# First modulation by output quarters, layer 0 queries and keys accumulated between them, second attention's scores two units ahead

## The reference, cut to what matters

```python
c_act = jax.nn.silu(c)
for l in range(DEPTH):                                   # DEPTH = 2
    mod = c_act @ ada_w[l] + ada_b[l]                    # [1024] @ [1024, 6144]
    sh_m, sc_m, g_m, sh_f, sc_f, g_f = jnp.split(mod[:, None, :], 6, axis=-1)
    h = _rmsnorm(x, norm_mix[l]) * (1 + sc_m) + sh_m
    proj = h @ w_in[l]                                   # queries qa, keys ka, values va, latents, gates, ...
    ...                                                  # attention with a table of relative biases,
    ...                                                  # latent attention, state space scan
    x = x + g_m * (merged @ w_out[l])
    h = _rmsnorm(x, norm_ffn[l]) * (1 + sc_f) + sh_f
    ...                                                  # gated feed-forward net with a convolution
# second block: two attentions with 8 heads of 64, then 32 experts, top 2 of one group, then a norm
```

## Time and profile before

| | |
|---|---|
| time, median of 3 runs | 1949.88 us (1947.15 to 1951.94) |
| the profiled execution's own time | 1946.01 us |
| its span in the profile | 1944.2 us |
| PE busy | 1864.6 us, 96% |
| DVE, ACT busy | 628.2 us (32%), 418.7 us (22%) |
| HBM read | 440.11 MB |
| mean granted PE clock | 0.983 |

### The profile page before, as it was taken

One profiled execution on the slowest core, in us unless ns is written; L12 is line 12 of the kernel. 1 busy time (PEld: TensorE's weight loads), 2 busy tenths in 40 slices (PEclk: granted clock), 3 DMA queues, 4 the chain that ended last, 5 costly groups with the idle time before them and its releaser, 6 DMA issues.

```text
span 1944.2 us, 20225 instructions
## 1 busy us (share of the span) xinstructions
PE 1864.6 (96%) x8628; PEld 1304.4 (67%) x8628; DVE 628.2 (32%) x1139; ACT 418.7 (22%) x888; POOL 0.8 (0%) x9
## 2 busy tenths in 40 slices
PE   6999999999999999999999999999889999999996
PEld 2477787888888648788888888865764444444432
DVE  4352267333232335127642232034441111111112
ACT  3253122212110234312212111012421011011112
POOL 0000000000000000000000000000000000000000
PEclk8999999999999999999999999999989999999999
DMA  9753364264446665337245453453329999999993
GB/s 388 266 168 125 130 218 154 105 216 156 147 161 229 215 216 174 130 111 274 92 161 185 132 171 136 141 216 130 135 82 406 428 428 427 427 427 427 428 427 128
DMA packets 137433, 443.25 MB, mean 228 GB/s; under 512 B 8832, under 2 KB 58240, under 8 KB 123520
## 3 DMA queue, kind: packets, MB, share of 16 engines
q1 hardware_dynamic: 134912, 438.26, 59.6%
q10 hardware_dynamic: 2432, 3.71, 0.6%
HBM read 440.11 MB, written 1.84 MB: 227 GB/s over the span
## 4 chain that ended last, share of the span: by engine, by line
PE 91%; DVE 4%; ACT 2%; DMA 1%; issue 1%; DVEq 1%; PEldq 0%; SPq 0%; ACTq 0%; PEld 0%
PE acc L705 36%; PE acc L1147 11%; PE acc L715 10%; PE aux L1186 6%; PE aux L980 4%; PE acc L980 4%; PE acc L1134 3%; PE acc L1001 3%; PE acc L1195 2%; PE aux L641 2%; PE aux L1195 2%; DMA ring<-in_ada_first 1%; PE acc L956 1%; PE aux L651 1%; PE aux L804 1%; ACT area L1269 1%
## 5 line engine op out<-in xcount | busy, mean ns | idle before, releaser
L705 PE MATMUL acc<-hT,ring 128*128 128x256 f32 x2688 | 592.2, 382 | 7.1 <-ACT hT L1342 7.1
L705 PEld LDWEIGHTS acc<-hT,ring 128*128 128x128 f32 x2688 | 513.2, 192 | 80.6 <-issue 12.0
L715 PE MATMUL acc<-ring,hT 128*128 128x512 f32 (+1 forms) x384 | 165.5, 591 | 5.3 <-ACT hT L1342 5.3
L1147 PE MATMUL acc<-ring,yT 128*64 128x512 f32 x512 | 169.2, 594 | 0.0
L2098 DVE SCALAR_TENSOR_TENSOR area<-acc,vectors,area 128x255 f32<-128x255 f32 (+1 forms) x176 | 72.7, 476 | 214.1 <-ACT area L1522 212.5
L715 PEld LDWEIGHTS acc<-ring,hT 128*128 128x128 f32 x384 | 73.7, 194 | 90.6 <-issue 88.4
L2336 DVE TENSOR_TENSOR xT<-xT,acc 128x1024 f32<-128x1024 f32 x17 | 20.8, 1222 | 292.3 <-PE acc L1195 292.3
L1724 DVE SCALAR_TENSOR_TENSOR ring<-ring,cspread 128x1024 f32<-128x1024 f32 x80 | 93.2, 1221 | 63.3 <-DMA ring<-in_ada_rest 63.3
L1147 PE MATMUL acc<-area,yT 128*64 128x512 f32 x384 | 112.9, 594 | 0.0
L1147 PEld LDWEIGHTS acc<-ring,yT 128*64 128x64 f32 x512 | 52.4, 137 | 74.5 <-issue 74.5
L1269 ACT ACTIVATE area<-aux 128x512 f32<-128x512 f32 (+3 forms) x65 | 41.4, 676 | 230.7 <-PE aux L641 225.1
(11 more groups left out here) (379 smaller groups left out, 1951.8 us busy)
## 6 DMA issues: line engine op xcount, KB each, us to landing
ring<-in_w_in SPq DMA_DIRECT2D x34, 2048.0 KB, 9.6
ring<-in_ffn_w_up SPq DMA_DIRECT2D x44, 1024.0 KB, 7.7
ring<-in_ada_rest SPq DMA_DIRECT2D x20, 2048.0 KB, 8.0
ring<-in_w_up SPq DMA_DIRECT2D x17, 2048.0 KB, 18.8
ring<-in_w_down SPq DMA_DIRECT2D x17, 2048.0 KB, 18.4
ring<-in_w_gate SPq DMA_DIRECT2D x16, 2048.0 KB, 15.6
area<-in_w_up SPq DMA_DIRECT2D x12, 2048.0 KB, 19.2
area<-in_w_down SPq DMA_DIRECT2D x12, 2048.0 KB, 17.8
```

Source lines behind the costliest of these rows:

```text
L705: mm = pe.matmul(acc[LU.buf[use]][:, SEQ * j:SEQ * j + SEQ], w[:, k, c0:c0 + P], x[:, k, :], start=(k == 0), stop=(k == n - 1))
L715: mm = pe.matmul(acc[LU.buf[use]][:, at:at + width], x[:, k, P * t:P * t + P], w[:, k, :], start=(k == 0), stop=(k == n - 1))
L1147: mm = pe.matmul(dst[CAP * e:CAP * e + CAP, :], xg[:, b, k, CAP * e:CAP * e + CAP], w[:, k, :], start=(k == 0), stop=(k == KT - 1))
```

## The change

Three parts.

1. `ada_first` is laid out anew so that its four loads split the *outputs*: load i has all eight input tiles for 256 columns of `sh_m` and the same 256 of `sc_m`. Each load so gives the shift and scale of feature tiles 2i and 2i + 1 by itself. PE's `first_block` has as many matmuls per load as before, into `aux2`, and a drain after each; `first_block_sums` has four matmuls of one column each per load, where there were four of four columns in all. DVE's `first_gains(i)` does copy, sums, gains and two tiles of `hT`; ACT's `first_shift(i)` adds two shifts.
2. The loads of `q` and `k` come between those of the first two blocks, in slots 2 and 3, and blocks 2 and 3 reuse slots 0 and 1 after blocks 0 and 1. `first_quarter(name, i)` accumulates input tiles 2i and 2i + 1 of `q` or `k` in their accumulators, in an order written out on PE among blocks, bias groups and sums. `v` and `ada4` are next in slots 0 and 1. The rest of `CHUNKS` keeps its order with the slots turned by two. The bias groups use `aux`, the first norm sum `acc[1]`. Two DMA issues of ACT (`rows`, `cspread`) move behind `first_shift(1)`. What ACT does after the last shift stays.
3. In the second attention PE issues `scores(u + 2)` after the transposes of unit u, where it issued `scores(u + 1)` ahead of them, and DVE takes the largest of unit u + 1 before it waits for the exponential of unit u.

```diff
-... "ada_first": ada_w[0, :, 0:4 * 512], ...
+... "ada_first": ada_w[0, :, 0:2 * D].reshape(KT, P, 2, ADA_AHEAD, 256).transpose(3, 1, 0, 2, 4).reshape(ADA_AHEAD, P, SLOT), ...
+FIRST_SLOT = (0, 1, 0, 1)
+Q_SLOT, K_SLOT = 2, 3
+CHUNKS = [(0, "v"), (0, "ada4")] + CHUNKS[4:]
...
+            first_load(0)
+            first_chunk("q", Q_SLOT)
+            first_load(1)
+            first_chunk("k", K_SLOT)
+            for i in range(2, ADA_AHEAD):
+                sp.wait_ge(early_full, i - 1)
+                first_load(i)
             for i, (l, name) in enumerate(CHUNKS):
                 s = i % SLOTS
-                if i < SLOTS:
-                    sp.wait_ge(*((part_ready, 3), (dn_done, 5), (part_ready, 4), (dn_done, 6))[i])
+                if i < 2:
+                    sp.wait_ge(early_full, i + 3)
+                elif i < SLOTS:
+                    sp.wait_ge(*release_of(0, ("q", "k")[i - 2]))
...
+            def first_block(i):
+                pe.wait_ge(landed[FIRST_SLOT[i]], 16 * (1 + i // 2))
+                if i:
+                    pe.wait_ge(early_out, i)
+                w = shaped(ring[:, FIRST_SLOT[i], :], KT, 512)
+                for k in range(KT):
+                    j = k % 4
+                    pe.matmul(aux2[32 * j:32 * j + 32, :], cwide[:, k, :], w[:, k, :], start=(k < 4), stop=(k >= 4))
+                pe.drain().then_inc(early_full, 1)
+            def first_block_sums(i):
+                pe.wait_ge(early_out, i + 1)
+                for j in range(4):
+                    at = KT * (j // 2) + 2 * i + j % 2
+                    mm = pe.matmul(pmod[:, at:at + 1], first_sums[:, P * j:P * j + P], ones[:, 0:1], start=True, stop=True)
+                mm.then_inc(ada_done, 1)
+            def first_quarter(name, i):
+                s, value = LAYER_RING[0, name]
+                pe.wait_ge(landed[s], value)
+                w, b = shaped(ring[:, s, :], KT, 512), LU.buf[name]
+                for t in range(T):
+                    for k in (2 * i, 2 * i + 1):
+                        pe.wait_ge(h_ready, k + 1)
+                        mm = pe.matmul(acc[b][:, 512 * t:512 * t + 512], hT[:, k, P * t:P * t + P], w[:, k, :],
+                                       start=(k == 0), stop=(k == KT - 1))
+                    if k == KT - 1:
+                        mm.then_inc(acc_full[b], 1)
...
+            first_block(0)
+            bias_group(0)
+            first_block_sums(0)
+            bias_group(1)
+            bias_group(2)
+            first_quarter("q", 0)
+            first_block(1)
+            bias_group(3)
+            first_block_sums(1)
+            first_quarter("q", 1)
+            first_quarter("k", 0)
+            first_quarter("k", 1)
+            first_block(2)
+            bias_group(4)
+            first_block_sums(2)
+            bias_group(5)
+            first_quarter("q", 2)
+            first_quarter("k", 2)
+            first_block(3)
+            first_block_sums(3)
+            first_quarter("q", 3)
+            first_quarter("k", 3)
...
+            take_bias(0)
+            take_bias(1)
+            first_shift(0)
+            take_bias(2)
+            take_bias(3)
+            first_shift(1)
             act.dma_start(rows..., a["spread"]...).then_inc(rows_in, 16)
+            act.dma_start(cspread, a["c"].to_broadcast([P, D])).then_inc(c_in, 16)
+            take_bias(4)
+            take_bias(5)
+            first_shift(2)
+            first_shift(3)
...
+            bias_steps(0, 4)
             dve.wait_ge(x_rt, 1)
             dve.reciprocal(rstd, rstd)
...
+            first_gains(0, 4, 5)
+            bias_steps(5, 8)
+            first_gains(1, 8, 9)
+            bias_steps(9, len(STEP_PIECES))
+            first_gains(2, 0, 0)
+            first_gains(3, 0, 0)
...
             scores(0)
             linear_transposes(0)
+            pe.wait_ge(acc_free[0], MU.turn["m_vb"] + 1)
+            scores(1)
             for u in range(8):
-                if u < 7:
-                    if u == 0:
-                        pe.wait_ge(acc_free[0], MU.turn["m_vb"] + 1)
-                    else:
-                        pe.wait_ge(p_exp, UNITS + u)
-                    if u == 3:
-                        pe.wait_ge(t2_out, 6)
-                    scores(u + 1)
                 pe.wait_ge(p_exp, UNITS + u + 1)
                 ...
                     transposes(...)
                 if u < 3:
                     linear_transposes(u + 1)
+                if u < 6:
+                    if u in (2, 3):
+                        pe.wait_ge(t2_out, u + 3)
+                    scores(u + 2)
...
+            largest(0)
             for u in range(8):
+                b = u % 2
+                if u < 7:
+                    largest(u + 1)
                 if u:
                     take_output(u - 1)
```

More of the change, by code:

```diff
@@ L167 @@
 W_SLOTS = 8
-RING_OF = (None, 3, 0, None, None, None, 1, 2)
+RING_OF = (None, 1, 2, None, None, None, 3, 0)
 PAIR_CHUNKS = 3 * AT_ONCE
@@ L195, with __init__ @@
 class Use:
-    def __init__(self, names, first=(0, 0), free=(1, 1)):
+    def __init__(self, names, first=(0, 0), free=(0, 0)):
         self.buf, self.full, self.turn = {}, {}, {}
@@ L644, in _, with norm_sum @@
             pe.wait_ge(fill, 1)
-            def norm_sum(before, squared=sqx):
+            def norm_sum(before, squared=sqx, dst=aux2):
                 for k in range(KT):
@@ L650, in norm_sum @@
                         pe.wait_ge(x_sq, 2 * before + k // 2 + 1)
-                    mm = pe.matmul(aux2[:, 0:SEQ], ones, squared[:, k, :], start=(k == 0), stop=(k == KT - 1))
+                    mm = pe.matmul(dst[:, 0:SEQ], ones, squared[:, k, :], start=(k == 0), stop=(k == KT - 1))
                 mm.then_inc(x_ss, 1)
-            norm_sum(0)
-            early = acc[0][:, 0:512]
+            norm_sum(0, dst=acc[1])
             def bias_group(g):
@@ L666, in bias_group @@
                         mm.then_inc(bias_full, 1)
-            pe.wait_ge(c_ready, 1)
[L669 to L679, removed]
+            def first_block(i):
[7 more added lines that the diff above has]
+                pe.drain().then_inc(early_full, 1)
@@ L1732, in _, with first_gains @@
             positions()
-            bias_steps(0, STEP_BUFFERS - 2)
+            bias_steps(0, 4)
             dve.wait_ge(x_rt, 1)
             dve.reciprocal(rstd, rstd)
-            bias_steps(STEP_BUFFERS - 2, len(STEP_PIECES))
+            def first_gains(i, first, last):
+                dve.wait_ge(early_full, i + 1)
+                dve.tensor_copy(first_sums, aux2).then_inc(early_out, 1)
+                bias_steps(first, last)
+                cc = cols[:, 0, :]
+                pairs = lambda x: shaped(x, 2, KT)[:, :, 2 * i:2 * i + 2]
+                dve.wait_ge(ada_done, i + 1)
+                tt(pairs(mod[:, 0:16]), pairs(pmod[:, 0:16]), pairs(cc[:, V_ADA:V_ADA + 16]), ALU.add)
+                D_()
+                stt(amix[:, 2 * i:2 * i + 2], mod[:, KT + 2 * i:KT + 2 * i + 2], 1.0, cc[:, V_NM + 2 * i:V_NM + 2 * i + 2], ALU.add, ALU.mult)
+                D_()
+                for k in (2 * i, 2 * i + 1):
+                    stt(hT[:, k, :], xT[:, k, :], amix[:, k:k + 1], rstd, ALU.mult, ALU.mult).then_inc(h_scaled, 1)
+            first_gains(0, 4, 5)
[4 more added lines that the diff above has]
+            first_gains(3, 0, 0)
             dve.wait_ge(rows_in, 16)
@@ L2189, in take_linear, with largest @@
                 dve.tensor_copy(dst[:, j0:j0 + 2, :], shaped(pmod, 2, SEQ)).then_inc(t2_out, 1)
-            for u in range(8):
+            def largest(u):
                 b, t = u % 2, u // 2 % 2
@@ L2200, in _ @@
                 dve.tensor_reduce(nmx[:, 4 * b:4 * b + 4], src, AX, ALU.max, negate=True).then_inc(s_max, 1)
+            largest(0)
+            for u in range(8):
+                b = u % 2
+                if u < 7:
+                    largest(u + 1)
                 if u:
```

71 lines of the change are left out of this document (35 added, 36 removed).

## The result

The changed kernel takes 1960.26 us (median of 5, 1955.86 to 1964.21) against 1947.44 us (median of 5, 1946.42 to 1951.94): ratio 1.0061, 95% interval 1.0045 to 1.0077. It is slower by some 12 us. The forecast was 1954.6, that is +4.7 on the 1949.9 of the kernel before, with a range to 1960.5. One execution of one experiment, the eight issues on SP, took 2833.49 us at a mean granted clock of 0.65 and is left out of its ratio.

A forecast was written before the change was run, and what follows sets the result against it. PE was taken to bound the start after 39.4 us, transfers the last 480 us. Parts 1 and 2 (+8.1) and part 3 (-3.4) gave +4.7 on 1949.9, so 1954.6, range 1946.5 to 1960.5.

The forecast's parts named there:

- The end passes shifts on: From the experts' start, transfers set the pace: the last 480 us cost the same, so earlier PE shifts pass one to one.
- PE's own work and the round trips: Start of layer 0: 44.8 us of work plus stalls between blocks, so `k` ends at 68.4 against 68.7.
- The wait that appears: Ahead of `v`: ACT's eight DMA issues delay its copy of `q`, so PE stands still 6.8 us, `v` starting at 75.2.
- The clock: At `v`: PE's stand drops the clock to half speed for some 3.2 us, losing 1.6 (bounds 0.8 and 2.5).
- the forecast's main case: Whole kernel: the clock falls only at `v`, the sum is +4.7, time 1954.6; chance 0.49.
- the early fall: Rival at the start: clock falls between 17.5 and 24.2, q0 up to 1.7 slower; +6.4 in all, 1956.3; chance 0.24.
- Part 3: Second attention from unit 4 on: 4.0 a unit instead of 4.9, unit 7 at 1381.6 instead of 1385.0: -3.4.
- +8.1: Start of the kernel, parts 1 and 2: `v` ends at 90.5 against 82.4.
- "same": Whole kernel: changed time within about 0.3%, 5.8 us, of the kernel before; chance 0.57.
- slower: Whole kernel: slower by more than about 0.3%, that is over 1955.7; chance 0.38.

The follow-up runs named there:

- the eight issues on SP: Changed kernel with the eight DMA issues of the bias table on SP instead of ACT; ratio 1.0033 to the kernel before, 1955.25 us.
- part 3 alone: Kernel before with only the changes to scores and largest in the second attention; ratio 0.9995, 1948.11 us.
- the other order: Changed kernel, issues on SP, 6 early idle-time matmuls, round trips of blocks 2 and 3 beside quarters; ratio 0.9998 to the kernel before, 1946.21 us.
- both: Changed kernel with the eight issues on SP and 10 idle-time matmuls around first and last sums; ratio 1.0025 to the kernel before, 1951.89 us.
- the version with all of it: The reordered changed kernel plus 4 idle-time matmuls ahead of q1 and 6 in the second attention; ratio 0.9969 to the kernel before, 1943.27 us.
- parts 1 and 2 alone: Changed kernel with the second attention's old loop of units; ratio 1.0064 to the kernel before, 1961.42 us.

## Why the prediction was right and where it was off

**The end passes shifts on.** Right. From the first expert's matmul to the end of the span it is 492.3 before and 494.0 in the changed kernel; in the profiles of the ten experiments it is 492.3 once and 493.9 to 494.1 nine times, though their first experts start up to 28 us apart (1444.0 to 1471.7). The 1.7 is one group of the last pass at the low clock, 3.6 instead of 1.92. What decides between the two values is not known; part 3 alone, with the start of before, has the longer one.

**PE's own work and the round trips.** The stalls stand where they were put: 1.4 and 1.5 around the first sums (2.1 and 1.6 forecast), 1.7 ahead of q1 (1.5), 1.2 ahead of q2 (1), 0.8 and 1.7 around the last sums (0.8 and 1.9). There are four such round trips, not the five that the forecast's text has. At the full clock `k` would have ended near 70.1: of the 5.8 us by which it ended later than forecast, 4.1 are the clock (0.9 in bias group 2, 1.5 in q0, 1.7 in q3 and k3), 1.7 are drains, starts, and quarters of 3.5 where 3.43 was taken. The experiment with the other order shows what the forecast only said, that the stalls come from late round trips: against "both", moving them beside quarters brought `k`'s end from 71.7 to 67.9, although fewer stalls were filled.

**The wait that appears.** Right in place, cause and order of size. From DVE's last tile (done 65.2) to `v` it is 12.8, forecast 14.1, since the eight issues took 6.4 and not 7.65. The stand itself is 3.8 and not 6.8, because q3 and k3 began late and ran slow beside ACT's chain. Putting the issues on SP removed the stand, the clock loss behind it, and 5.5 us of the time: this cause is shown. The rule of the Trainium skill about issue time (DMA: Bandwidth & Descriptors, Issuing engines are not separate DMA queues) speaks of one DMA; each of these took 0.6 to 1.1 here, against a median of 6.3 and 6.9 us from issue to landing, so for one DMA the trace agrees. It is eight in a row, on an engine that others wait for, that make 6.4.

**The clock.** Here the forecast's main case was wrong: it took the early fall as a rival at 0.24, and it came (1956.3 was that rival's time). It also left out a third fall, after block 3's round trip (1.7), which came in the shadow of the stand. `v` paid 1.8 for the fall that was forecast at 1.6 (13.9 with the issues on SP, 15.7 here). The forecast likened this start to the kernel that the Trainium skill describes (TensorE: Matmul & The Clock Gate, HAM oscillation), in which every burst comes in at the low clock. The trace agrees only in part: the clock fell, but q1, k0 and k1, behind a stop of 1.7, ran at the full one. Idle-time matmuls brought q0 back to the full clock in all four profiles that have them there (3.70, against 5.2 to 5.6 in the three without), and q3 with k3 in both that have them there, so PE's idleness is shown as the cause of these falls; where the gap ahead of q1 stayed open the clock fell behind it, and with that gap filled too (the version with all of it) q1 was back at 3.67.

**Part 3.** The size was off: -3.4 forecast, -0.2 in the profile, and -1.0 (-2.5 to +0.8) for part 3 alone. The mechanism is right: unit 7's values end 41.6 after the first scores where they took 42.1, in spite of 3.4 lost to the low clock in units 6 and 7. All six profiles with part 3 and no filling there have this fall, at the same place; with six idle-time matmuls it is gone and the values end at 39.2, so the worth of the order is 2.9 where the clock holds. The forecast left out that the old order can lose its clock as well, as the profile of parts 1 and 2 alone shows; against that the worth is 3.2 even with the fall. One more step of the forecast was off: units 1 and 2 take 4.76 each where 4.4 was taken, with a wait of 0.23 ahead of the linear transposes, as DVE's `take_linear` now stands behind the largest of the next unit.

**The sum.** Forecast +8.1 and -3.4; in the profile +11.3 and -0.2, and +3.1 in other places, 1.7 of it the clock in the last pass. The measured 1960.26 is under the range's upper end by 0.24 us, and that is luck: the kernel before came out at 1947.44 and not at 1949.9, so the change cost 12 us where the forecast said 4.7 and its range ended at 10.6. The forecast also gave "same" (within 0.3%) 0.57 and slower 0.38, and slower came. What was right is the sign, the place of the stalls and the wait for ACT; what it lacked is a price for the clock wherever it counted a stall.

**What stays open.** What puts an execution of the kernel before into the long group. The old order's loss of the clock in unit 7 (3.0) and the last pass (1.7) together make 4.7, which is the distance of the groups' medians on the first chip (1946.4 and 1951.1), but no long execution of it was profiled. How much of the 1.4 between `v` and the second attention belongs to the change: this stretch takes 1262.2 to 1267.8 in the twelve profiles, so 1.4 may be none of it.

## What to carry to other kernels

When work is moved ahead of a chain, ask what the work used to cover: here the copy of `q` sat behind eight DMA issues on ACT, which 13.7 us of `k` hid, and moving `k` forward laid them bare. Splitting one long wait into short ones multiplies the round trips between engines; each must be laid beside work that does not depend on it. Here the order that does so brought 4.8 us in the profile, and the split itself is not shown to bring anything. Where PE stalls of more than a microsecond follow each other closely, add a term for the work behind them at half the clock, with a chance, for some such stalls cost it here and others of the same length did not. Look for the same instruction at two durations in the timeline: that is where the clock fell. And before the profile of one execution is taken as the base of a sum, see whether the single executions lie in groups.

## What the runs showed of the hardware

The clock fell after less idleness in one piece than the trace of before had shown. There it had come after 2.8 us without work; in the changed kernel PE worked 1.9, 1.1, 1.1 and 1.2 us with stops of 1.4 and 1.5 among them from 14.9 to 23.0, and the granted clock was 0.80 from 20 to 22 us and 0.50 from 22 us on; in the second attention one stop of 1.1 and one of 0.34 preceded it.

It did not fall at every such stop. Behind 1.23 us without work, ahead of q2, the quarters ran at the full clock (7.10); behind 1.7, ahead of q1, they took 10.54 in the profile of the changed kernel and 13.53 in that of the same start with the old order of units. In the old order itself unit 7's values took 1.97 behind a wait of 1.51 for its transposes, and 3.65 behind one of 1.86.

Matmuls that nobody reads, 6 of 0.43 us in the attention with part 3, took 3.5 us off the stretch from the first scores to the first expert, and the executions of that version lie within 2.6 us where those of the kernel before lie within 7.5.
